# The second expert's first products ahead of the first expert's turns, in a bank of their own

## What is computed

```python
a = jnp.einsum('sd,edf->sef', hr, w_gate)      # 32 experts, d = 1024, f = 256
u = jnp.einsum('sd,edf->sef', hr, w_up)
act = jax.nn.silu(a) * u * gate[:, :, None].astype(hr.dtype)
return jnp.einsum('sef,efd->sd', act, w_down)
```

## Time and profile before

| | us |
|---|---|
| median of 3 runs | 938.74 |
| lowest and highest | 938.4, 938.83 |
| span of the profiled execution, first to last instruction | 936.9 |
| TensorE busy in the span | 928.0 |
| VectorE busy | 743.2 |
| ScalarE busy | 625.6 |

### The profile page before, as it was taken

One profiled execution on the slowest core, in us unless ns is written; L12 is line 12 of the kernel. 1 busy time (PEld: TensorE's weight loads), 2 busy tenths in 40 slices (PEclk: granted clock), 3 DMA queues, 4 the chain that ended last, 5 costly groups with the idle time before them and its releaser, 6 DMA issues.

```text
span 936.9 us, 13599 instructions
## 1 busy us (share of the span) xinstructions
PE 928.0 (99%) x5025; PEld 803.9 (86%) x5025; DVE 743.2 (79%) x1111; ACT 625.6 (67%) x953; POOL 20.6 (2%) x41
## 2 busy tenths in 40 slices
PE   9999999999999999999999999999999999999997
PEld 7888888888888888888888899999998888888886
DVE  6668686678999999999999889888887655555576
ACT  6685686676778788778778775847574544434456
POOL 2500000000000000000000000000000000000000
PEclk9999999999999999999999999999999999999999
DMA  9855427523799999999999364837457566555531
GB/s 340 243 183 187 147 91 261 171 63 135 259 365 377 362 361 384 350 354 373 342 367 322 103 211 138 263 115 228 156 184 243 178 201 198 182 183 179 183 132 45
DMA packets 102766, 214.50 MB, mean 229 GB/s; under 512 B 5672, under 2 KB 60480, under 8 KB 97088
## 3 DMA queue, kind: packets, MB, share of 16 engines
q1 hardware_dynamic: 101072, 211.70, 65.5%
q0 software_dynamic: 1344, 2.01, 0.8%
q10 hardware_dynamic: 304, 0.20, 0.1%
HBM read 212.84 MB, written 1.05 MB: 228 GB/s over the span
## 4 chain that ended last, share of the span: by engine, by line
PE 94%; DMA 2%; POOL 2%; DVE 1%; SPq 0%; ACT 0%; issue 0%; DVEq 0%; ACTq 0%
PE bank L2363 20%; PE bank L2361 20%; PE bank L2362 20%; PE bank L3194 6%; PE bank L3193 6%; PE bank L3192 6%; PE bank L2378 4%; PE bank L2374 2%; PE bank L2368 2%; PE bank L2369 1%; DMA x<-in_x_dram 1%; PE bank L2714 1%; DMA pos_i<-in_positions_dram 1%; PE bank L3218 0%; PE bank L3219 0%; PE bank L3220 0%
## 5 line engine op out<-in xcount | busy, mean ns | idle before, releaser
L2361 PE MATMUL bank<-w_hi,xT_hi 128*128 128x512 f32 (+2 forms) x594 | 234.3, 395 | 0.0
L2363 PE MATMUL bank<-w_hi,xT_lo 128*128 128x512 f32 (+2 forms) x594 | 229.9, 387 | 0.0
L2362 PE MATMUL bank<-w_lo,xT_hi 128*128 128x512 f32 (+2 forms) x594 | 229.7, 387 | 0.0
L465 DVE TENSOR_TENSOR w_lo<-stage,w_hi 128x1024 fp32r<-128x1024 f32 (+3 forms) x94 | 107.5, 1143 | 30.3 <-ACT w_hi L451 28.8
L2363 PEld LDWEIGHTS bank<-w_hi,xT_lo 128*128 128x128 f32 x594 | 111.6, 188 | 22.7
L2361 PEld LDWEIGHTS bank<-w_hi,xT_hi 128*128 128x128 f32 x594 | 112.1, 189 | 20.7 <-DVE w_lo L467 0.2
L2362 PEld LDWEIGHTS bank<-w_lo,xT_hi 128*128 128x128 f32 x594 | 111.8, 188 | 20.8
L3192 PE MATMUL bank<-xT_hi,w_hi 128*128 128x256 f32 x440 | 124.5, 283 | 0.0
L3193 PE MATMUL bank<-xT_lo,w_hi 128*128 128x256 f32 x440 | 124.5, 283 | 0.0
L3194 PE MATMUL bank<-xT_hi,w_lo 128*128 128x256 f32 x440 | 124.5, 283 | 0.0
L451 ACT ACTIVATE w_hi<-stage 128x1024 fp32r<-128x1024 f32 (+3 forms) x96 | 95.5, 995 | 31.6 <-PE bank L2363 13.3
(11 more groups left out here) (492 smaller groups left out, 1578.2 us busy)
## 6 DMA issues: line engine op xcount, KB each, us to landing
stage<-in_w_in_dram SPq DMA_DIRECT2D x36, 1024.0 KB, 5.2
stage<-in_w_gate_up_dram SPq DMA_DIRECT2D x44, 512.0 KB, 4.7
stage<-in_expert_w_gate_dram SPq DMA_DIRECT2D x33, 512.0 KB, 5.5
stage<-in_expert_w_up_dram SPq DMA_DIRECT2D x33, 512.0 KB, 6.4
second<-in_expert_w_down_dram SPq DMA_DIRECT2D x16, 1024.0 KB, 6.9
stage<-in_expert_w_down_dram SPq DMA_DIRECT2D x15, 1024.0 KB, 6.7
stage<-in_w_down_dram SPq DMA_DIRECT2D x11, 1024.0 KB, 4.7
stage<-in_w_out_dram SPq DMA_DIRECT2D x8, 1024.0 KB, 5.8
```

Of the source, the lines that this page charges most:

```text
L465: nc.vector.tensor_tensor(w_lo[:, s, 0:half], src[:, 0:half], w_hi[:, s, 0:half].bitcast(F32), ALU.subtract)
L2361: mm(o, k_hi, v_hi, start=start, stop=False)
L2362: mm(o, k_hi, v_lo, start=False, stop=False)
L2363: return mm(o, k_lo, v_hi, start=False, stop=stop)
```

## The change

The first half of expert 1's columns, 12 products, moves from behind the turns of expert 0 to ahead of them, at the end of step 0, and goes to bank 3. The second half of these columns goes to bank 3 too, and ScalarE and VectorE read that expert's columns from there. TensorE waits for the first `hidden` no more before expert 1's columns. The four products with zeros are gone; the first products of the return of group 0 start the sums of banks 0 to 3. For that, TensorE's steps of group 0 are written out (`peeled=1`), and its loop runs over groups 1 and 2.

```diff
-    def expert_steps(eng, groups, step, tail, straight=False):
+    def expert_steps(eng, groups, step, tail, straight=False, peeled=0):
...
-            with eng.Fori(0, groups - 1) as g:
+            for g in range(peeled):
+                for j in range(2, PER_GROUP + 2):
+                    step(g, j)
+            with eng.Fori(peeled, groups - 1) as g:
...
+    def expert_columns(g, j, st):
+
+        return bank[3 if st is main and isinstance(g, int) and (g, j) == (0, 1) else 6]
...
-                nc.scalar.activation(silu_t[:, 0], bank[6][:, 0:FF], ACT.Tanh,
+                nc.scalar.activation(silu_t[:, 0], expert_columns(g, j, st)[:, 0:FF], ACT.Tanh,
...
-                stt(silu_g[:, 0], silu_t[:, 0], 1.0, bank[6][:, 0:FF], ALU.add, ALU.mult).then_inc(sem("expert_silu"), 1)
+                columns = expert_columns(g, j, st)
+                stt(silu_g[:, 0], silu_t[:, 0], 1.0, columns[:, 0:FF], ALU.add, ALU.mult).then_inc(sem("expert_silu"), 1)
...
-            def columns_of(half, u0, g):
+            def columns_of(half, u0, g, j):
                 pe.wait_ge(st.lo_ready, g * PER_TURN + (u0 + 1))
-                s = u0 % RING
+                s, o = u0 % RING, expert_columns(g, j, st)[:, :]
...
-                        mm(bank[2 * c + t][:, :], tokens[t], y_hi[:, c], start=False, stop=False)
+                        mm(bank[2 * c + t][:, :], tokens[t], y_hi[:, c], start=isinstance(g, int) and g == 0, stop=False)
...
-            def open_sums(banks):
-
-                for n in banks:
-                    mm(bank[n][:, :], zeros[:, 0:P], slot_of[:, 0], start=True, stop=False)
-
             def gate_up(g, j):
-                if j:
+                second = isinstance(g, int) and (g, j) == (0, 1)
+                if j and not second:
                     pe.wait_ge(sem("expert_hidden"), eighths(g, j))
...
-                columns_of(0, gate_unit(base, j), g)
+                if not second:
+                    columns_of(0, gate_unit(base, j), g, j)
...
                 if j == PER_GROUP + 1:
+                    if isinstance(g, int) and g == 0:
+                        pe.wait_ge(sem(name + "_slot_gates"), 2)
                     bring_back(g)
                 if j:
                     down(g, j - 1, up_unit(base, j) + 1)
-                    if j == 1:
-                        pe.wait_ge(sem(name + "_slot_gates"), 2)
-                        open_sums((0,))
...
                     turn_gates(range(1, groups))
-                    open_sums((1, 2, 3))
+                    columns_of(0, gate_unit(base, 1), g, 1)
                 turn_hidden(g, j)
...
-            expert_steps(pe, groups, step, tail)
+            expert_steps(pe, groups, step, tail, peeled=1)
```

More of the change, by code:

```diff
@@ L2090, in hidden_low @@
                 dve.wait_ge(sem("expert_tanh"), eighths(g, e0 + j + 1))
-                stt(silu_g[:, 0], silu_t[:, 0], 1.0, bank[6][:, 0:FF], ALU.add, ALU.mult).then_inc(sem("expert_silu"), 1)
+                columns = expert_columns(g, j, st)
+                stt(silu_g[:, 0], silu_t[:, 0], 1.0, columns[:, 0:FF], ALU.add, ALU.mult).then_inc(sem("expert_silu"), 1)
                 dve.wait_ge(sem("expert_silu"), eighths(g, e0 + j + 1))
-                stt(hidden[:, 0], bank[6][:, FF:2 * FF], slot_gates[:, bass.ds(gate_column(g, j), 1)], silu_g[:, 0],
+                stt(hidden[:, 0], columns[:, FF:2 * FF], slot_gates[:, bass.ds(gate_column(g, j), 1)], silu_g[:, 0],
                     ALU.mult, ALU.mult).then_inc(sem("expert_hidden"), 1)
@@ L2887, in first_columns @@
                     ins.then_inc(st.unit_done, 1)
-            def columns_of(half, u0, g):
+            def columns_of(half, u0, g, j):
                 pe.wait_ge(st.lo_ready, g * PER_TURN + (u0 + 1))
-                s = u0 % RING
+                s, o = u0 % RING, expert_columns(g, j, st)[:, :]
                 for k in range(4):
                     kk = 4 * half + k
-                    ins = three(bank[6][:, :], xg_hi[:, kk], xg_lo[:, kk], w_hi[:, s, 512 * k:512 * k + 512],
+                    ins = three(o, xg_hi[:, kk], xg_lo[:, kk], w_hi[:, s, 512 * k:512 * k + 512],
                                 w_lo[:, s, 512 * k:512 * k + 512], start=kk == 0, stop=kk == KD - 1)
@@ L2967, in gate_up @@
                     return
-                columns_of(0, gate_unit(base, j), g)
+                if not second:
+                    columns_of(0, gate_unit(base, j), g, j)
                 if j == PER_GROUP:
                     pe.wait_ge(sem(name + "_moved"), g * 2 + 2)
-                columns_of(1, up_unit(base, j), g)
+                columns_of(1, up_unit(base, j), g, j)
             def step(g, j):
```

## The result

The changed kernel takes **945.08 us** (median of 5 runs, 943.89 to 946.16) against 938.67 us (5 runs, 938.4 to 938.83): a ratio of 1.0067 [1.0056, 1.0077]. It is 6.4 us slower, where 1.8 us were forecast. Its profiled execution took 945.39 us, with a span of 943.5, 6.6 longer than before.

The account below looks back on a forecast made before the run. TensorE, running dense, was taken to bound the kernel. The late down weights and `hidden` gave a net +1.8 us, the removed 1.18 us already inside: 938.74 + 1.8 = 940.5 us, with 939.6 to 941.5 holding about 0.8.

Parts of the forecast that it names:

- Steps 1 to 5: At the first expert's turns: twelve moved products delay `aT_hi` by 1.88 us; TensorE then waits 2.2 us for down weights.
- step 6: After the wait for down weights: twelve products run to 258.8; the third expert's columns start 1.75 us later.
- the term of nothing for the unrolled group: TensorE's written-out group 0: bounded by 0.12 us either way a time, counted as nothing.
- the second rival: In the new wait for down weights the clock falls to 1.2 GHz, 2.8 us more: 943.0; chance 0.05.
- Step 7: At the fourth expert (j = 3), the last tight one: turns at 276.14, slip 1.81 us; net +1.8 us.
- The third rival: Group 0's unrolled instructions must be fetched, up to 0.12 us a time over eight experts: 940.5 to 941.5; chance 0.05.
- The criterion I had given for it: Sign of the third rival in the trace: experts of group 0 that take over 8.5 us.
- 1.18 us at most: Four zero products removed: 0.94 us from 247.78 to 248.72 with the wait in it, and 0.24 at 257.25.

Follow-up runs that it names:

- the runs with and without filling: Changed kernel with groups 0 and 1 written out: with eight zero products ahead of the first down products 940.68 us, without them 941.65 us.
- the run with its wait of 2.29 us and the clock at 1.00: Changed kernel with the first expert's down weights split ahead of `aT_hi` and `aT_lo`: 942.13 us, profiled execution 940.38 us.
- the padded kernel before: Kernel before with never-executed clearing products added to the jumped-over overflow code: 52 more took 940.33 us, 60 more took 942.81 us.

## Why the prediction was wrong, step by step

**Steps 1 to 5 hold.** The moved products began at 247.73 (247.90 forecast), the turns at 250.59 (250.72), `aT_hi` at 251.02 (251.14), the down weights were ready at 254.60 + 1.22 = 255.82 (255.94), TensorE began on them at 255.88 (256.00) after 2.01 us (2.2). The constant difference of 0.1 is there from the start of the stretch on.

Two steps failed: step 6, on the clock behind the wait, and the term of nothing for the unrolled group. Together they are 4.4 of the 4.6 us between 940.5 and 945.08.

**Step 6 failed.** "Twelve down products take it to 258.8": they took it to 260.32, at the lower clock. `hidden` was ready at 258.94 as forecast, and did not decide. The slip of 1.75 was 2.83. That was the second rival, given 0.05 and priced at 2.8 us, of which 0.3 were to hide, by all twelve products at 0.47. About eight ran low, at 0.43, and part of the loss lies in what would have been a wait for `hidden`: it cost 0.97 us by the runs with and without filling. The chance was too small. I had only the row behind the last product and set against it that a pause between dense stretches is another case. The Trainium skill (TensorE: Matmul & The Clock Gate, "What's actually happening") lets the clock fall only after a whole stretch of idleness. The runs disagree: behind a wait of 0.8 us, and behind this one of 2.0 us, TensorE was at work again when the clock fell.

**Step 7 holds** once the clock does: with the wait filled the fourth expert's turns stand at 276.27 (276.14 forecast), and the kernel is 1.97 us slower (1.8 forecast).

**"The unrolled first group: take nothing"** was the costliest failure: it measured 3.4 us. I looked for its price per round of the loop and within the loop, and found none. Its price lies 270 us later, at a jump that the change does not touch, and the page's instruction queue, 26 transfers, was there to be read. The third rival named the Trainium skill's rule on branches and applied it to the loop's own. It is not a cost of written-out code at all (two groups written out: 1.0001 [0.9992, 1.001]). The criterion I had given for it, experts of group 0 over 8.5 us, would have missed it.

**"1.18 us at most"** for the zero products was an upper bound and fits only as that. Three of them cost nothing, since they stood in the wait for `hidden`. Without them the time is 940.0 us or more in five of eleven executions, with the profiled clock at 0.50; with them and the same two groups written out all ten lie from 938.6 to 939.4. So they kept the clock up besides.

The sum of 6.4 us, then: queue slip 1.97, clock behind the first wait 0.97, placement 3.4. Of the last, 2.2 are the wait and the rest the clock behind it, as the run with its wait of 2.29 us and the clock at 1.00 shows. Likewise a wait of 1.53 us with the clock kept cost 940.33 - 938.87 = 1.5 in the padded kernel before; one of 2.28, where the run's mean clock fell to 0.996 or 0.997, cost 942.81 - 938.81 = 4.0. The three parts are successive differences of medians, so their sum closes by construction; each is good to a few tenths. Left open is what exactly decides in which executions the clock falls behind a short wait.

## What to carry to other kernels

Work moved ahead of an engine's hand-over is late for every engine that serves its queue in order behind that hand-over: follow the slip to the next margin (0.47 us here) before counting any gain. Products that look useless may fill a wait and so keep the clock up; price a wait with the products behind it at the lower level as well (1.0 to 1.5 us here). And when a change alters the length of an engine's program, look behind each later jump for a wait that "issue" released, and for the instruction queue's transfers among the DMAs; its cost is one of placement, which an unrelated shift of the code brings or takes away.

## What the runs showed of the hardware

- Behind one jump over skipped code TensorE showed no wait in some kernels, and a wait released by "issue" of 1.53, 2.24 to 2.29, 3.03 or 4.67 to 4.89 us in others, that ended 4.5 to 4.9 us after the last product ahead of the jump. Edits that only moved the code brought the wait, shifted it and took it away. That it is a wait for code is inferred from the transfer 2.5 to 2.7 us before its end.
- The granted clock fell to 0.50 behind waits of 0.8, 2.0, 2.2, 2.3 and 3.0 us after TensorE had resumed; in one execution it fell inside a wait of 2.29 us, ahead of its end, and so it did in the waits of 4.67 to 4.89 us. Products of 512 columns were then spaced 0.43 us instead of 0.23.
- It did not fall behind every such wait: in the profiled execution with the down weights split early it read 1.00 throughout behind a wait of 2.29 us, and by their times only some executions have the fall behind waits of 0.8 and 2.1 us.
- Eight products of zeros in such a wait kept the clock at 1.00 and made the kernel 0.97 us faster.
